# Shift of the first context tile as added products, with the modulation weights loaded in two halves

## The reference, cut to what matters

```python
m = silu(cond) @ w_mod + b_mod            # six parts of 1024: shift, scale, gate, ...
h = rmsnorm(x, g) * (1.0 + scale) + shift # scale, shift: one row for all tokens
z = h @ w_in                              # latent and context tokens, same weights
cq, ckv, kr, qs, ks, vs = split(z)
kv = (rmsnorm(ckv, g_kv_a) @ w_ukv)       # keys and values from the compressed keys ckv
```

## Time and profile before

| what | value |
|---|---|
| median of 3 runs (lowest to highest) | 1366.16 us (1365.88 to 1367.72) |
| the profiled execution's own time | 1368.26 us |
| span of its records | 1366.3 us |
| mean granted clock of TensorE, share of full speed | 0.991 |
| PE / DVE / ACT / POOL busy, share of the span | 97% / 75% / 54% / 37% |

### The profile page before, as it was taken

One profiled execution on the slowest core, in us unless ns is written; L12 is line 12 of the kernel. 1 busy time (PEld: TensorE's weight loads), 2 busy tenths in 40 slices (PEclk: granted clock), 3 DMA queues, 4 the chain that ended last, 5 costly groups with the idle time before them and its releaser, 6 DMA issues.

```text
span 1366.3 us, 19011 instructions
## 1 busy us (share of the span) xinstructions
PE 1322.1 (97%) x7118; PEld 1117.9 (82%) x7118; DVE 1022.2 (75%) x1396; ACT 737.3 (54%) x1405; POOL 510.9 (37%) x350
## 2 busy tenths in 40 slices
PE   4899998999999999999999999999999999999998
PEld 0688887889888988898888888888888888888886
DVE  1888777787788777776687796767687776868678
ACT  2756565788877877984223543444353535344440
POOL 2567664021199995411000031404123232404333
PEclk8999999999999999999999999999999999999999
DMA  9565657633156564401334535527261735437053
GB/s 375 181 179 167 176 162 236 200 91 88 27 214 194 154 206 153 107 16 32 93 108 139 174 103 213 189 94 265 83 236 62 250 121 213 157 125 245 31 185 124
DMA packets 149130, 210.55 MB, mean 154 GB/s; under 512 B 10136, under 2 KB 101144, under 8 KB 146224
## 3 DMA queue, kind: packets, MB, share of 16 engines
q1 hardware_dynamic: 144432, 200.91, 45.4%
q10 hardware_dynamic: 4352, 8.39, 1.7%
q0 software_dynamic: 256, 0.05, 0.0%
HBM read 162.90 MB, written 44.32 MB: 152 GB/s over the span
## 4 chain that ended last, share of the span: by engine, by line
PE 73%; DVE 15%; ACT 7%; DMA 2%; issue 1%; SPq 0%; DVEq 0%; ACTq 0%
PE f_ps L2749 19%; PE f_ps L2712 17%; PE a_ps L1449 7%; PE o_ps L1797 6%; PE a_ps L1465 5%; PE a_ps L1495 5%; PE f_ps L2280 5%; ACT s_pr L1546 3%; DVE s_nmx L1631 2%; PE t_ps L977 2%; DMA t_wm<-in_w_mod 1%; PE t_ps L966 1%; PE f_ps L2765 1%; PE t_ps L992 1%; DVE f_fin L2557 1%
## 5 line engine op out<-in xcount | busy, mean ns | idle before, releaser
L2260 POOL TENSOR_TENSOR f_wr<-f_wr,f_wr 128x1024 f32<-128x1024 f32 x24 | 61.8, 2576 | 286.1 <-DMA f_wr<-in_w_mlp 157.3
L2749 PE MATMUL f_ps<-f_bh,f_ah 128*128 128x512 f32 x392 | 152.6, 389 | 0.6 <-DVE mix L2583 0.6
L2749 PE MATMUL f_ps<-f_bh,f_al 128*128 128x512 f32 x392 | 152.5, 389 | 0.0
L2749 PE MATMUL f_ps<-f_bl,f_ah 128*128 128x512 f32 x392 | 152.5, 389 | 0.0
L1645 DVE TENSOR_TENSOR l_pT<-a_ps,l_pT 128x512 fp32r<-128x512 f32 (+1 forms) x192 | 109.0, 594 | 53.2 <-ACT l_pT L1556 53.1
L2581 DVE TENSOR_TENSOR mix<-mix,f_ps 128x512 f32<-128x512 f32 x180 | 116.5, 682 | 37.5 <-PE f_ps L2749 37.2
L1449 PE MATMUL a_ps<-l_k,l_q 96*128 96x512 f32 (+1 forms) x576 | 136.4, 366 | 0.5 <-DVE l_mo L1657 0.5
L977 PE MATMUL t_ps<-w_in,t_h 128*128 128x416 f32 (+2 forms) x600 | 123.8, 352 | 0.0
L1556 ACT ACTIVATE l_pT<-a_ps 128x512 fp32r<-128x512 f32 (+1 forms) x192 | 95.0, 525 | 39.6 <-PE a_ps L1465 39.2
L1563 ACT ACTIVATE l_pr<-a_ps,l_nb 128x256 f32<-128x256 f32 (+1 forms) x128 | 100.5, 790 | 12.5 <-DVE l_nb L1636 10.2
L1449 PEld LDWEIGHTS a_ps<-l_k,l_q 96*128 96x128 f32 x576 | 95.3, 189 | 12.5 <-DVE l_mo L1657 0.7
(11 more groups left out here) (252 smaller groups left out, 2951.2 us busy)
## 6 DMA issues: line engine op xcount, KB each, us to landing
f_hq<-scratch_hs SPq DMA_DIRECT2D x64, 512.0 KB, 5.4
l_wg<-in_w_mod SPq DMA_DIRECT2D x8, 2048.0 KB, 8.4
f_w<-in_w_mlp SPq DMA_DIRECT2D x16, 1024.0 KB, 7.5
f_ring<-scratch_hs SPq DMA_DIRECT2D x32, 512.0 KB, 5.2
f_wr<-in_w_mlp SPq DMA_DIRECT2D x24, 512.0 KB, 3.8
t_wm<-in_w_mod SPq DMA_DIRECT2D x8, 1024.0 KB, 13.0
scratch_k<-t_kT SPq DMA_DIRECT2D x20, 384.0 KB, 3.7
l_k<-scratch_k SPq DMA_DIRECT2D x8, 960.0 KB, 10.3
```

What stands on the lines that cost most here:

```text
L2749: last = nc.tensor.matmul(ps[:, b, :], op_a[s][x][:, f, t * P:(t + 1) * P], op_b[s][w][:, f, :], start=(i in (M1, M2, M5) and f == 0 and k ...
```

## The change

It does seven things, all in the token phase.

1. `w_mod` is loaded in eight transfers of 1024 KB again, but each holds two blocks of 128 rows x 1024 columns: four with the scale columns at the front of the queue, four with the shift columns behind the norms. Tile 0's rows, `a0`, `a1` and tile 1's rows lie between them, so ahead of the shift.
2. PE makes the scale with two products for each k (j = 2, 3), and the shift (j = 0, 1) only behind `project_first`. Each half has its own eight steps.
3. Tile 0 is multiplied by norm and scale only. Its first 16 products run without the shift; the 8 low ones follow the shift's modulation.
4. The shift row of the context is turned into columns (`turn_shift`, four transposes), split in a high and a low part (`t_shift_col`, 128 x 8), and added to z as 24 products (`shift_first`) whose stationary operand is one column seen 128 times.
5. Scale rows are spread and copied first (rows 0 to 3), shift rows later (4 to 7), ahead of `shift_first` on PE. `spread_row` reads 64 partitions instead of 128.
6. DVE makes `r0` low ahead of the bias for the shift; `lo_fill("c", i)` of context tiles stands ahead of `low_vs`.
7. ACT splits `r1` together with `r2` and `r3` behind tile 2's fills; `uq` is loaded only when the shift's modulation is through (`wm_used` at 16).

```diff
@@ sync
-        for k in range(KC - 2):
-            load_wm(k)
+        for n in range(4):
+            load_pair(n, slice(D, 2 * D), wm_scale[:, 2 * n:2 * n + 2, :])
         load_x(0)
-        load_wm(KC - 2)
-        load_wm(KC - 1)
         load_raw("a0")
+        load_raw("a1")
         load_x(1)
-        load_raw("a1")
...
+        for n in range(4):
+            load_pair(4 + n, slice(0, D), wm_near[:, 2 * n:2 * n + 2, :] if n < 3 else wm_far[:, :, :])
         load_raw("kv")
         load_raw("r0")
...
+        sp.wait_ge(wm_used, 2 * KC)
         load_raw("uq")
@@ gpsimd, add_shift
             if t == 1:
-                pool.wait_ge(spread_copied, 4)
+                pool.wait_ge(spread_copied, 6)
@@ scalar
         high_weights("a0")
-        square_x(1, stx[:, 1:2])
-        high_weights("a1")
         hi_fill("x0", 0)
         hi_fill("x1", 0)
+        high_weights("a1")
+        copy_spread(0)
...
+        square_x(1, stx[:, 1:2])
         root_x(1)
-        for n in range(4):
-            copy_spread(n)
         high_weights("kv")
         high_weights("r0")
+        act.wait_ge(turned_shift, TURNED0 + 1)
+        nc.scalar.activation(shift_col[0][:, :].rearrange("p (j c) -> p j c", j=2), shift_view(), ACT.Copy).then_inc(shift_hi, 1)
+        for n in range(4, 8):
+            copy_spread(n)
...
-            if i == 1:
-                high_weights("r1")
...
             if i == 1:
+                high_weights("r1")
                 high_weights("r2")
                 high_weights("r3")
@@ vector
+        dve.wait_ge(wm_used, KC)
+        link(V.tensor_tensor(mo[64:P, :], ps[64:P, UB, :], bm[64:P, :], ALU.add))
+        V.tensor_tensor(mo[64:P, :], mo[64:P, :], gm[64:P, :], ALU.mult).then_inc(mod_ready, 1)
         inverse_x(0)
...
         low_weights("kv")
+        low_weights("r0")
+        dve.wait_ge(wm_used, 2 * KC)
+        V.tensor_tensor(mo[0:64, :], ps[0:64, UB, :], bm[0:64, :], ALU.add).then_inc(mod_ready, 1)
+        dve.wait_ge(shift_hi, HI0 + 1)
+        V.tensor_tensor(shift_col[1][:, :].rearrange("p (j c) -> p j c", j=2), shift_view(),
+                        shift_col[0][:, :].rearrange("p (j c) -> p j c", j=2).bitcast(F32), ALU.subtract).then_inc(shift_lo, 1)
         for i in range(NT + 1):
...
+            if i < NCT:
+                lo_fill("c", i)
             if i < NT:
                 low_vs(i)
@@ tensor
+        def turn_shift():
+            for c in range(4):
+                last = nc.tensor.transpose(ps[:, UB, 64 * c:64 * c + 64], mo[0:64, c * P:(c + 1) * P], ident[0:64, 0:64])
+            last.then_inc(turned_shift, 1)
+
+        def shift_first():
+            pe.wait_ge(shift_lo, LO0 + 1)
+            for k in range(KC):
+                for i, (a, x) in enumerate(((0, 0), (0, 1), (1, 0))):
+                    ins = MM(ps[:, ZB, 0:NA], shift_col[a][:, k:k + 1].to_broadcast([P, P]), w_in[x][:, k, 0:NA],
+                             start=False, stop=(k == KC - 1 and i == 2))
             ins.then_inc(z_ready, 1)
...
+        project_first()
+        for k in range(KC):
+            pe.wait_ge(wm_loaded[4 + k // 2], 16)
+            modulation(k, (0, 1), wm_shift(k))
+        project_first_low()
+        pe.wait_ge(mod_ready, 2)
+        turn_shift()
+        for n in range(4, 8):
+            spread_row(n)
+        shift_first()
```

More of the change, by code:

```diff
@@ L146, in token_phase @@
     zs = room("t_z", [P, IN_W])
-    wm_in = {i: Z.room(at, skip)(f"t_wm{i}", [P, n, 2 * D]) for i, at, skip, n in ((0, "H", 0, 4), (4, "L", 0, 3), (7, "T", 9984, 1))}
-    wm = [wm_in[i][:, k - i, :] for k in range(KC) for i in (0, 4, 7) if 0 <= k - i < (4, 0, 0, 0, 3, 0, 0, 1)[i]]
+    wm_scale = Z.room("H")("t_wm_scale", [P, KC, D])
+    wm_near = Z.room("L")("t_wm_near", [P, KC - 2, D])
+    wm_far = Z.room("T")("t_wm_far", [P, 2, D])
+    wm_shift = lambda k: wm_near[:, k, :] if k < KC - 2 else wm_far[:, k - KC + 2, :]
     room = Z.room("L", 6144)
@@ L177, in token_phase @@
     small = Z.small
+    shift_col = [small(f"t_shift_col{i}", [P, KC], F32R) for i in range(2)]
     stx = small("t_stx", [P, 2])
@@ L723, in modulate_first @@
                 x = xr[:, 0, f * BANK:f * BANK + BANK]
[L724 to L728, removed]
+                dve.wait_ge(spread, f + 1)
+                V.scalar_tensor_tensor(out=x, in0=x, scalar=stx[:, 0:1], in1=ps[:, spread_bank[f], :],
+                                       op0=ALU.mult, op1=ALU.mult).then_inc(h0_ready, 1)
         def low_weights(j):
@@ L868, in vector @@
         lo_fill("x1", 0)
+        low_weights("a1")
         inverse_x(1)
-        low_weights("a1")
         scale_x(1)
@@ L1007, in up_kv, with modulation @@
                 ins.then_inc(u_ready, 1)
[L1009 to L1013, removed]
+        def modulation(k, js, w):
+            for j in js:
+                last = MM(ps[32 * j:32 * j + 32, UB, :], silu[:, k, :], w[:, j % 2 * BANK:(j % 2 + 1) * BANK],
                           start=(k == 0), stop=(k == KC - 1))
             last.then_inc(wm_used, 1)
-        pe.wait_ge(ident_loaded, 16)
-        pe.wait_ge(mod_ready, 1)
         def spread_row(n):
[L1021 to L1024, removed]
+            r, j = 1 - n // 2 % 2, (2 if n < 4 else 0) + n % 2
+            if n >= 4:
+                pe.wait_ge(spread_copied, n - 3)
+            rows = slice(64 * (j // 2), 64 * (j // 2) + 64)
+            MM(ps[:, spread_bank[n], :], ident[rows, 32 * j + r:32 * j + r + 1].to_broadcast([64, P]), mo[rows, :],
                start=True, stop=True).then_inc(spread, 1)
[L1027 to L1030, removed]
         def project_first():
@@ L1042, in project_first @@
                     pe.wait_ge(w_lo, 1)
-                ins = MM(ps[:, ZB, 0:NA], hT[0][:, k, :], w_in[1][:, k, 0:NA], start=False, stop=(k == KC - 1))
-            ins.then_inc(z_ready, 1)
-        project_first()
+                MM(ps[:, ZB, 0:NA], hT[0][:, k, :], w_in[1][:, k, 0:NA], start=False, stop=False)
+        def turn_shift():
[8 more added lines that the diff above has]
+                             start=False, stop=(k == KC - 1 and i == 2))
+            ins.then_inc(z_ready, 1)
+        pe.wait_ge(silu_ready, 1)
+        for k in range(KC):
+            pe.wait_ge(wm_loaded[k // 2], 16)
+            modulation(k, (2, 3), wm_scale[:, k, :])
+        pe.wait_ge(ident_loaded, 16)
+        pe.wait_ge(mod_ready, 1)
+        spread_row(0)
+        spread_row(1)
+        fill("x0", 0)
+        fill("x1", 0)
+        spread_row(2)
+        spread_row(3)
+        project_first()
+        for k in range(KC):
+            pe.wait_ge(wm_loaded[4 + k // 2], 16)
[6 more added lines that the diff above has]
+        shift_first()
         for i in range(NT + 1):
@@ L1098, in token_phase @@
     b = Bag()
-    b.spent = {"exped": (exped, 1), "silu": (silu_ready, 1), "mod": (mod_ready, 1), "gains": (gains_scaled, 1),
-               "low": (first_low, 1), "spread": (spread, 8), "copied": (spread_copied, 8), "used": (wm_used, KC)}
+    b.spent = {"exped": (exped, HI0 + 1), "silu": (silu_ready, TURNED0 + 1), "mod": (mod_ready, 2), "gains": (gains_scaled, LO0 + 1),
+               "low": (first_low, 1), "spread": (spread, 8), "copied": (spread_copied, 8), "used": (wm_used, 2 * KC)}
     b.spent_loads = ([raw_loaded[j] for j in JOBS], wm_loaded, 16)
```

36 lines of the change are left out of this document (14 added, 22 removed).

## The result

The changed kernel took 1371.61 us (median of 11 runs, 1369.54 to 1377.62), the kernel before 1366.29 (11 runs, 1365.20 to 1368.43): a ratio of 1.0046 [1.0035, 1.0057]. Slower, as forecast, and the median is 0.6 us from the forecast of 1371.0. The 11 runs are not one cluster: seven lie from 1369.54 to 1372.27, four from 1375.65 to 1377.62. That split into a lower and an upper cluster is what the forecast did not have, and most of the experiments are about it.

A forecast was written before the change was run, and what follows sets the result against it. PE, busy for 97% of the span, was taken as the bound. 3.1 us late at tile 3's square plus 1.7 for the clock gave 4.8 slower: 1371.0 us against the median of 1366.16, range 1366.4 to 1377.0.

The forecast's parts named there:

- PE bounds and an early offset stays: Whole span: PE is busy for 97% of it, so whatever the start gains or loses stays in the total.
- The scale at 17.5, a half step without halving: Scale modulation: through at 17.5, 11 us before the old end, with a two-product step priced at 1.06 us, not halved.
- The shift's arrival at 32.6: Shift loads: the last pair arrives at 32.6, two steps end at 34.7, the 8 low products at 36.4.
- `r0` ends the wait: PE's wait from 36.4: r0 lands at 35.6, high half 1.50, low half 1.97, bias 0.69, done 39.8; turn 0.4.
- z at 48.7 without the clock: Tile 0's z: four spreads (3.59 us) and 24 products (4.82) end at 48.7, late by 5.6 us.
- `t_vs` at 0.30: DVE, from z to tile 1's projection: t_vs takes 0.30 us, not 1.91, since POOL's add is over by 47.
- Tile 1 to tile 3, gain given back: ACT, tiles 1 to 3: r1's gain ahead is paid back behind by three splits (1.43 us more); square 3.1 late.
- The clock, +1.7 behind the gap: PE after 3.4 us without work: spreads and 24 products run 3.0 us at half speed, losing 1.5; 1.7 with edges.
- Rival 1: The clock holds, if PE, slower in its first steps, fills the gap up to 39.8: +3.1, 1369.3; chance 0.20.
- Rival 2: Delay paid back: DVE's halves of uq no longer collide with POOL's add, 2 us return: +1.1, 1367.3; chance 0.12.
- Rival 3: Faster: DVE paces the stretch and its list is 3.6 us shorter, if z comes by 43.1: 1362.6; chance 0.12.
- Rival 4: Low clock through the shift's steps, with half-array steps leaving it low: products end at 57, +11.3, 1377.5; chance 0.06.

The follow-up runs named there:

- number 1: The changed kernel with DVE making r0 low behind the shift's bias and column split, not ahead of them: 1371.05 us, ratio 1.0031 to the kernel before.
- number 6: The changed kernel with six identity products on PE behind the scale and fourteen more behind the low products: 1371.71 us, ratio 1.0036 to the kernel before.
- number 2: The changed kernel with the last two spreads (latent shift rows) behind the 24 products, their copies behind tile 0's squares: 1373.51 us, ratio 1.0046 to the kernel before.
- number 5: The changed kernel with six identity products on PE in its idle time behind the scale: 1376.30 us, ratio 1.0070 to the kernel before.
- number 4: The changed kernel with ACT's split of r1 back ahead of tile 1's compressed keys: 1373.92 us, ratio 1.0055 to the kernel before.
- number 8: The kernel before the change, with four identity products behind each modulation step (eight behind the sixth): 1365.03 us, ratio 0.9987 to the kernel before.
- number 7: The changed kernel with r0's low half behind the shift and six identity products behind the scale: 1368.92 us, ratio 1.0018 to the kernel before.
- numbers 3: The changed kernel with only 3 of the 24 shift products, the rest of the shift left out: 1367.30 us, ratio 1.0015 to the kernel before.

## Why the prediction was right, and where it was not

- **PE bounds and an early offset stays: right.** From the square of tile 3 to the span's end before took 1303.9 us, the changed kernel 1304.4, its two further profiles 1303.0 and 1306.0. The rest is unchanged to within its own scatter.
- **The scale at 17.5, a half step without halving: right.** 17.4. A step of one k took 1.91 / 2 = 0.96 us, and 5.34 / 6 = 0.89 without gaps. Two products fewer for each k saved about a tenth, not half.
- **The shift's arrival at 32.6: early by up to 1.6.** Where PE was quick its last steps began between 32.62 (number 1) and 34.21 (number 6). It was hidden behind DVE's list in each.
- **`r0` ends the wait: right as a mechanism.** ACT could take it at 36.10 to 37.35, not at 35.6; 1.5 for the high half, 1.76 for the low one (I had 1.97), 0.68 for the bias, 0.29 for the turn (I had 0.4). Numbers 2, 5 and 6 show the bias behind `r0` as PE's releaser.
- **z at 48.7 without the clock: a little early.** 49.96 in number 6, 1.3 later, because ACT took `r0` 1.75 us later. Its square of tile 3, 66.64, is 4.25 late where the sum had 3.1.
- **4.4 us from z's products to tile 1's projection: right**, 53.55 - 49.28 = 4.3.
- **`t_vs` at 0.30: right**, 0.28. POOL's add ran from 43.61 to 45.99, ahead of it, and took 2.38 us instead of 3.44, as if each had held up the other before. The Trainium skill, "SBUF — State Buffer", section "SBUF: two separate sides", has it as a lock held for a whole instruction; the trace agrees (1.91 us beside the add, 0.28 after it).
- **Tile 1 to tile 3, gain given back: right.** The keys' high part 1.53 us behind z's copy (I had 1.6), three splits 4.23 us instead of 2.85, and number 4's square at the same time.
- **The clock, +1.7 behind the gap: the step that failed.** In the three profiles of the changed kernel the clock fell after the idle stretch of 1.68 us behind the scale, which the forecast did not look at. PE then fills the gap by being slow, z is at 49.4, and the time is about that of number 6, where the clock does not fall. In the other branch the gap opens, and the low clock behind it costs 4.6 us (number 6 against number 5), not 1.7. I priced a low stretch of 3.0 us, the length in the earlier trace rows; here it was 10 us long, and all of it is on the path.
- **The number: in part luck.** In the lower cluster the 1.7 is not paid. Without it the sum is 3.1; the profile is 0.45 us above that at the square of tile 3 (its z products end at 49.28, not 48.7) and another 0.45 behind it, 4.0 in all, and the median of the seven lower runs is 1370.62. The four upper runs carry the median of all to 1371.61. The base helped too: the sum was made from a profile that had paid for a low clock itself (number 8), and then set on a median 2.1 us below that profile.
- **Rival 1** (PE, slower in its first steps, fills the gap) is what the three profiles show, by a mechanism the rival didn't name: it needs the low clock early. Its +3.1 was +3.55 at tile 3. **Rival 2** did not happen: DVE's halves of `uq` took 3.96 us again (76.15), beside POOL's add (75.98). **Rival 3**'s condition, z by 43.1, was met by no run of the new order. **Rival 4** did not happen: the clock was back at 31 in the first profile, before the shift's steps began at 31.88, and stood at 1.00 through these steps in every profile. Whether such steps leave a low clock low was therefore not put to the test.
- The upper cluster of the changed kernel, 1375.65 to 1377.62, was seen in no profile of it. That it is the branch with the gap is inferred, not shown: number 5, which forces that branch, has all its runs from 1375.04 to 1376.84, number 2 has the gap without a filler at 1375.60, and the upper cluster is absent from the five runs of number 6 and the eleven of number 7. 1377.62 needs some of the later scatter too.

Why the change loses is shown by numbers 1, 3, 6 and 8. Before, scale and shift came with the same eight loads, DVE added the shift to tile 0's rows ahead of the products, and 16 + 8 products made z. Now z waits for `r0`'s split, a turn, four spreads and 24 added products, in a row, behind the shift's loads. The scale is there 11 us earlier, which nothing on this path can use.

## What to carry to other kernels

A load brought forward is worth only what its last consumer can start earlier: write down the chain behind the load that now comes last, with each engine's in-order list in it. Ask of each idle stretch of PE what runs behind it: the low clock behind a wait of 1.7 us, over covered work, cost about 0.6 us here; behind one of 3.5 us, over work on the path, it cost 4.6 us beyond the wait itself. Before a profile serves as the base of a sum, look for a low clock in it. A few products with the identity in such waits are a cheap test, and in the kernel before they were also the better change (1366.99 to 1365.03 us, ratio 0.9987 [0.9978, 0.9996]).

## What the runs showed of the hardware

- The idle time of 1.7 us behind the scale was followed by the low clock in some executions of the same program and not in others. The changed kernel fell to 1.2 GHz between 20.8 and 21.3 us in three profiles of three, numbers 3 and 4 at about 21.5 and 19.9; numbers 1 and 2, whose programs are the same up to there, stayed at 2.4 (16 products in 3.29 us).
- Low stretches differ in length: some 10 us in the changed kernel (20.8 to 31), in number 2 and in number 5 (42 to 52, with PE busy throughout), but only from about 59.3 to 62.7 in the kernel before.
- The column of the granted clock does not show all of it. In the kernel before it reads 1.00 in every microsecond from 6 to 17, yet the first three steps (6.98, 10.64, 12.84) took 1.93 to 1.94 us each, and the next, at 15.33, 1.06.
- With six identity products of 128 columns in the 1.7 us (numbers 5 to 7), and with four to eight between the steps (number 8), the stretches that followed show 1.00. The Trainium skill, "TensorE: Matmul & The Clock Gate", section "Why this matters for your kernels", advises against idle gaps between bursts; the trace agrees, with the low clock behind a gap of 1.68 us in five profiles of seven.
- A quicker engine can make a kernel slower: number 5 took off no work and added six products, and all its five runs lie at the change's upper cluster, by opening the gap behind which the clock is low.
